# Gate and up projections as seven block products, with two low parts and all weight sums on GpSimd

## What is computed

```python
def conv_ffn(h, prev, w_gate, w_up, conv_w, conv_b, w_down):
    g = h @ w_gate
    gp = jnp.concatenate([prev.astype(g.dtype), g], axis=1)
    c = conv_b
    for j in range(CONV_W):
        c = c + conv_w[j] * gp[:, j:j + t]
    y = (jax.nn.gelu(c) * (h @ w_up)) @ w_down
    return y, gp[:, t:]
```

## Time and profile before

| | |
|---|---|
| median of 3 runs | 2069.16 us (2069.08 to 2069.41) |
| profiled execution | 2069.33 us, of which its span 2067.5 us |
| PE / PE weight load busy | 2038.8 us (99%) / 1797.0 us |
| DVE / ACT / POOL busy | 981.7 us (47%) / 763.9 us (37%) / 198.6 us (10%) |
| mean DMA rate | 106 GB/s |

### The profile page before, as it was taken

The page is one execution under the profiler, slowest core; times in us unless marked ns, Lnnn a source line. Parts: engine busy times, 40 slices in busy tenths (PEclk is TensorE's granted clock), DMA queues, the critical chain, the costliest instruction groups (busy, mean ns, idle before and its releaser), DMA issues.

```text
span 2067.5 us, 30583 instructions
## 1 busy us (share of the span) xinstructions
PE 2038.8 (99%) x12398; PEld 1797.0 (87%) x12398; DVE 981.7 (47%) x1648; ACT 763.9 (37%) x1318; POOL 198.6 (10%) x458
## 2 busy tenths in 40 slices
PE   9999989999999999999999999999999999999997
PEld 7889767987789999999989888799778999999996
DVE  5453664435444443443453467653545444343443
ACT  4222552435344233232244447243534433223232
POOL 3012121000100000000010124210010000000001
PEclk9999999999999999999999999999999999999999
DMA  5324143245622122222221211723572222212221
GB/s 176 124 79 149 52 162 129 92 152 187 243 85 83 62 82 83 91 69 62 76 77 62 82 55 34 275 77 117 197 285 85 65 79 82 78 56 82 82 82 55
DMA packets 111066, 219.42 MB, mean 106 GB/s; under 512 B 7011, under 2 KB 52367, under 8 KB 110862
## 3 DMA queue, kind: packets, MB, share of 16 engines
q1 hardware_dynamic: 91234, 148.00, 21.4%
q0 software_dynamic: 19696, 69.47, 9.9%
HBM read 200.51 MB, written 18.24 MB: 106 GB/s over the span
## 4 chain that ended last, share of the span: by engine, by line
PE 95%; DVE 2%; ACT 2%; issue 1%; DMA 0%; POOL 0%; SPq 0%; DVEq 0%; ACTq 0%; POOLq 0%
PE bank L794 15%; PE bank L796 15%; PE bank L795 15%; PE bank L858 7%; PE bank L860 7%; PE bank L862 7%; PE bank L859 5%; PE bank L861 5%; PE bank L863 5%; PE bank L820 1%; PE bank L1240 1%; PE bank L1256 1%; PE bank L1197 1%; PE bank L1282 1%; PE bank L1293 1%
## 5 line engine op out<-in xcount | busy, mean ns | idle before, releaser
L2093 DVE TENSOR_TENSOR w_lo<-raw,w_hi 128x1024 fp32r<-128x1024 f32 x265 | 319.2, 1220 | 508.9 <-ACT w_hi L1563 505.0
L1563 ACT ACTIVATE w_hi<-raw 128x1024 fp32r<-128x1024 f32 x265 | 275.1, 1054 | 254.6 <-PE bank L796 203.5
L794 PE MATMUL bank<-w_hi,hT_lo 128*128 128x512 f32 x720 | 290.7, 404 | 3.1 <-DVE w_lo L2093 1.9
L858 PE MATMUL bank<-hT_hi,w_lo 128*128 128x384 f32 (+1 forms) x856 | 290.1, 339 | 0.0
L860 PE MATMUL bank<-hT_lo,w_hi 128*128 128x384 f32 (+1 forms) x856 | 289.3, 338 | 0.0
L862 PE MATMUL bank<-hT_hi,w_hi 128*128 128x384 f32 (+1 forms) x856 | 289.3, 338 | 0.0
L796 PE MATMUL bank<-w_hi,hT_hi 128*128 128x512 f32 x720 | 281.9, 391 | 0.0
L795 PE MATMUL bank<-w_lo,hT_hi 128*128 128x512 f32 x720 | 281.2, 391 | 0.0
L859 PE MATMUL bank<-hT_hi,w_lo 128*128 128x256 f32 (+1 forms) x856 | 239.0, 279 | 0.0
L861 PE MATMUL bank<-hT_lo,w_hi 128*128 128x256 f32 (+1 forms) x856 | 239.0, 279 | 0.0
L863 PE MATMUL bank<-hT_hi,w_hi 128*128 128x256 f32 (+1 forms) x856 | 239.0, 279 | 0.0
(11 more groups left out here) (372 smaller groups left out, 2997.4 us busy)
## 6 DMA issues: line engine op xcount, KB each, us to landing
raw<-w_ffn_gate SPq DMA_DIRECT2D x44, 512.0 KB, 4.1
raw<-w_ffn_up SPq DMA_DIRECT2D x44, 512.0 KB, 5.1
raw<-w_ffn_down SPq DMA_DIRECT2D x22, 1024.0 KB, 4.9
kcX<-cache_mem_k POOLq DMA_DIRECT2D x16, 1024.0 KB, 6.1
vcX<-cache_mem_v POOLq DMA_DIRECT2D x16, 1024.0 KB, 6.9
raw<-w_in_even SPq DMA_DIRECT2D x13, 1024.0 KB, 5.6
raw<-w_in_odd SPq DMA_DIRECT2D x12, 1024.0 KB, 5.2
raw<-w_cq SPq DMA_DIRECT2D x8, 1024.0 KB, 7.5
```

What stands on the lines that cost most here:

```text
L794: pe.matmul(out, wl, xh, start=first, stop=False)
L858: pe.matmul(oa, wl, hT_hi[:, k, 0:HA], start=f, stop=False)
L1563: act.activation(w_hi[:, g % W_SLOTS, 0:n], raw[:, q % 2, UNIT * i:UNIT * i + n], ACT.Copy).then_inc(*hi_made.mark(c, u))
L2093: dve.tensor_tensor(w_lo[:, s, 0:n], raw[:, q % 2, UNIT * i:UNIT * i + n], flat(w_hi[:, s, 0:n]), ALU.subtract).then_inc(*lo_made.mark(c, u))
```

## The change

The operands of gate and up are seen as 2 x 2 blocks. The weights of a pair are cut by their input rows (k = 0 to 3, and 4 to 7) and by output tile (f even, f odd); the tokens are cut into the first 320 (`HT`) and the last 320. A scheme of seven products (Strassen's identity in its form with seven products and shared sums) takes the place of the eight. Seven weight units stand for each pair where there were four: A11, A12, A22 are blocks of the loaded weights (`quarter`), and S1 to S4 are sums and differences that POOL forms in fp32 (`weight_sum`), S1 into a buffer of its own and the others in place in `raw`. Each unit is used for gate and for up, with four row blocks each: 7 x 2 x 4 x 3 = 168 matmuls of 320 columns, in 14 banks. ACT still makes all high parts. POOL makes the low parts of S1 and S3 (`weight_low`), DVE those of the other five.

The token side has sums as well, made once in each layer before and during pair 0: t1 and t2 (on DVE) and t3 and n4 (on POOL), each split into high and low. The outputs come back by additions: ACT copies the banks of A11 and A12, POOL adds these two (`first_corner`, "C11"), and DVE makes the rest with `to_sums`, `c22`, `c12` and `c21`, each operation with one operand in PSUM. Now `af` holds up and is multiplied by `cv` in place (`gated`). `FFN_PLAN` sets pairs and groups in the order gu0 gu1 dn0, gu2 gu3 dn1, gu4 gu5 dn2, gu6 gu7 dn3, gu8 gu9 gu10 dn4 dn5. The tiles of pair 0 no longer stand between the last norms; `gate_up` has two transposes between its first banks.

```diff
+FFN_PLAN = [("gu", 0), ("gu", 1), ("dn", 0)]
+for _g in range(1, GROUPS - 2):
+    FFN_PLAN += [("gu", 2 * _g), ("gu", 2 * _g + 1), ("dn", _g)]
+FFN_PLAN += [("gu", FT // 2 - 3), ("gu", FT // 2 - 2), ("gu", FT // 2 - 1), ("dn", GROUPS - 2), ("dn", GROUPS - 1)]
+
+PARTS = ("A11", "A12", "S1", "S2", "S3", "S4", "A22")
+POOL_PARTS = ("S1", "S3")
+HT = TOK // 2
+A_SLOTS = 6
...
-                    sp.wait_ge(*lo_made.at(oc, ou + on - 1))
+                    sp.wait_ge(*lo_made.at(oc, PARTS.index("A22" if ou else "S4") if oc[0] == "gu" else ou + on - 1))
+                    if oc[0] == "gu" and ou == 0:
+                        sp.wait_ge(*lo_pool.at(oc, PARTS.index("S3")))
...
+                def weight_sum(j, part):
+
+                    c = ("gu", l, j)
+                    q0, q1 = LOAD_OF[(c, 0)][0], LOAD_OF[(c, 2)][0]
+                    s1 = sum_at[1 if j else 0][:, :, :]
+                    if part == "S1":
+                        pool.wait_ge(*w_in[q0 % 2].at(q0))
+                        pool.wait_ge(*w_in[q1 % 2].at(q1))
+                        if j == 1:
+                            pool.wait_ge(*xn_made.at(f"ffn{l}", T - 1))
+                        out, a, b, op = s1, quarter(c, 0, 1), quarter(c, 1, 1), ALU.add
+                    elif part == "S3":
+                        out, a, b, op = quarter(c, 0, 1), quarter(c, 0, 0), quarter(c, 0, 1), ALU.subtract
+                    elif part == "S2":
+                        pool.wait_ge(*lo_made.at(c, PARTS.index("A11")))
+                        pool.wait_ge(*pool_done.at("sum", l, j, "S3"))
+                        out, a, b, op = quarter(c, 0, 0), s1, quarter(c, 0, 0), ALU.subtract
+                    else:
+                        pool.wait_ge(*lo_made.at(c, PARTS.index("A12")))
+                        pool.wait_ge(*pool_done.at("sum", l, j, "S2"))
+                        out, a, b, op = quarter(c, 1, 0), quarter(c, 1, 0), quarter(c, 0, 0), ALU.subtract
+                    pool.tensor_tensor(out, a, b, op).then_inc(*pool_done.mark("sum", l, j, part))
+
+                def weight_low(j, part):
+
+                    c, u = ("gu", l, j), PARTS.index(part)
+                    w = FIRST_UNIT[c] + u
+                    lo, hi = (t[:, w % W_SLOTS, :].rearrange("p (q n) -> p q n", n=P) for t in (w_lo, w_hi))
+                    pool.wait_ge(*hi_made.at(c, u))
+                    pool.tensor_tensor(lo, part_source(c, u), hi.bitcast(F32), ALU.subtract).then_inc(*lo_pool.mark(c, u))
...
+                def first_corner(j, key):
+
+                    pool.wait_ge(*lin_a.at(("gu", l, j), (key, "A12")))
+                    dst = gp[0][:, HALO:HALO + HT] if key == "g" else af[0][:, 0:HT]
+                    pool.tensor_tensor(dst, dst, p1[key][:, :], ALU.add).then_inc(*pool_done.mark("C11", l, j, key))
...
+                norm_rstd(f"ffn{l}", [0])
+                norm_rstd(f"ffn{l}", [1])
+                weight_sum(0, "S1")
+                norm_rstd(f"ffn{l}", [2])
+                weight_sum(0, "S3")
+                norm_rstd(f"ffn{l}", [3])
+                weight_sum(0, "S2")
+                norm_rstd(f"ffn{l}", [T - 1])
+                weight_low(0, "S1")
+                weight_sum(0, "S4")
+                pool.wait_ge(*act_done.at("hF", l, T - 1, 1))
+                pool.tensor_tensor(t3F[:, :, :], hF[:, 1, :, HT:TOK], hF[:, 0, :, HT:TOK], ALU.subtract).then_inc(*pool_done.mark("t3F", l))
+                weight_low(0, "S3")
+                pool.wait_ge(*dve_done.at("t2F", l, 1))
+                pool.tensor_tensor(hF[:, 1, :, 0:HT], hF[:, 1, :, 0:HT], t2F[:, :, :], ALU.subtract).then_inc(*pool_done.mark("n4F", l))
+                pool.wait_ge(*act_done.at("prevT", l))
+                for j in range(FT // 2):
+                    more = j + 1 < FT // 2
+                    halo(2 * j)
+                    halo(2 * j + 1)
+                    if j:
+                        weight_low(j, "S3")
+                    first_corner(j, "g")
+                    first_corner(j, "u")
+                    if more:
+                        weight_sum(j + 1, "S1")
+                        weight_sum(j + 1, "S3")
+                    tails(2 * j)
+                    if more:
+                        weight_sum(j + 1, "S2")
+                        weight_low(j + 1, "S1")
+                    tails(2 * j + 1)
+                    if more:
+                        weight_sum(j + 1, "S4")
...
+                def gate_up(j, between={}):
+
+                    c = ("gu", l, j)
+                    for u, part in enumerate(PARTS):
+                        wait_unit(c, u)
+                        if j == 0:
+                            wait_operand(part)
+                        hi, lo = operand[part]
+                        for m, key in enumerate("gu"):
+                            out = lin.open(pe, c, (key, part))
+                            for k in range(KT // 2):
+                                cols = slice(P * (2 * k + m), P * (2 * k + m) + P)
+                                ins = three(out[:, 0:HT], weight(c, u, False)[:, cols], weight(c, u, True)[:, cols], lo[:, k, :], hi[:, k, :],
+                                            k == 0, k == KT // 2 - 1)
+                            ins.then_inc(*lin_full.mark(c, (key, part)))
+                            if (part, key) in between:
+                                between[part, key]()
...
-                for g in range(GROUPS):
-                    for j in group_pairs(g):
-                        c = ("gu", l, j)
-                        for e in range(2):
-                            if j == 0 and e == 0:
-                                continue
-                            cols_tile(c, f"ffn{l}", P * e, ("g", e))
-                            cols_tile(c, f"ffn{l}", 256 + P * e, ("u", e), last=e == 1)
-                    if g:
+                for kind, i in FFN_PLAN[:-1]:
+                    if kind == "gu":
+                        gate_up(i, {("A11", "g"): lambda: norm_tile(nm, T - 2), ("A12", "g"): lambda: norm_tile(nm, T - 1)} if i == 0 else {})
+                    else:
                         for t in range(T):
-                            down(g - 1, t)
+                            down(i, t)
...
+                        if oc[0] == "gu":
+                            act.wait_ge(*lin_full.at(oc, ("u", PARTS[ou])))
...
+                    if f is not None:
+                        gelu(f)
+                    refill_hi(g0 + 4)
+                    if i:
+                        first_product(i, "g")
+                    if f is not None:
+                        gelu(f + 1)
+                    if i:
+                        first_product(i, "u")
+                    if f is not None:
+                        high_a(f)
+                    corner(i, "g")
+                    refill_hi(g0 + 5)
+                    if f is not None:
+                        high_a(f + 1)
+                    corner(i, "u")
+                    if i == 0:
+                        high_t("t3", t3[0][:, :, :], t3F[:, :, :], 0, pool_done.at("t3F", l))
+                    refill_hi(g0 + 6)
+                    if i == 0:
+                        high_t("n4", n4[0][:, :, :], hF[:, 1, :, 0:HT], 0, pool_done.at("n4F", l))
+                    refill_hi(g0 + 7)
+                    refill_hi(g0 + 8)
+                    refill_hi(g0 + 9)
+                    tap0(2 * i)
+                    refill_hi(g0 + 10)
+                    tap0(2 * i + 1)
...
+                def to_sums(j, key):
+
+                    c = ("gu", l, j)
+                    dve.wait_ge(*pool_done.at("C11", l, j, key))
+                    dve.wait_ge(*lin_full.at(c, (key, "S2")))
+                    dve.tensor_tensor(u2[key][:, :], p1[key][:, :], lin.bank(c, (key, "S2"))[:, 0:HT], ALU.add).then_inc(*lin_v.mark(c, (key, "S2")))
+                    dve.wait_ge(*lin_v.at(c, (key, "S2")))
+                    dve.tensor_tensor(p1[key][:, :], u2[key][:, :], lin.bank(c, (key, "S1"))[:, 0:HT], ALU.add).then_inc(*lin_v.mark(c, (key, "S1")))
...
+                sum_t(0)
+                low_ts(0)
+                sum_t(1)
+                low_ts(1)
+                halves(nm, T - 1)
+                for n, (kind, i) in enumerate(FFN_PLAN):
+                    c = (kind, l, i)
+                    g0 = FIRST_UNIT[c]
+                    f = 2 * FFN_PLAN[n - 1][1] if n and FFN_PLAN[n - 1][0] == "gu" else None
+                    if f is not None:
+                        c21(i_before, "u")
+                        taps(f + 1)
+                        gated(f)
+                    if kind == "dn":
+                        if f is not None:
+                            refill_lo(g0 + 4)
+                            low_a(f)
+                            gated(f + 1)
+                            low_a(f + 1)
+                        down(i)
+                        continue
+                    refill_lo(g0 + 4)
```

(24 more changed lines are left out.)

375 lines of the change are left out of this document (277 added, 98 removed).

## The result

The changed kernel takes 2138.42 us (median of 4 runs, 2137.19 to 2139.61), the kernel before 2069.12 on the same chip. The ratio is 1.0337, 95% interval 1.0319 to 1.0355: 69 us slower. The forecast was 2050, the range 2006 to 2084.

The account below looks back on a forecast made before the run. PE, busy 99% of the span, was taken to bound the kernel. From 2069.3 us, 77 came off for less PE work and 59 were added for waits (29.4 a layer), giving 2051, stated as 2050; range 2006 to 2084.

Parts of the forecast that it names:

- start of the FFN (pair 0): Before pair 0: norm scale, transposes and t1 no longer hidden; PE waits 6.5 us a layer, bounds 3 and 9.
- gu3, gu5, gu7, gu9: Second pairs behind a `down`: late sums and low parts make PE wait 2.4 us each, 9.6 a layer.
- gu10: The one third pair behind a `down` in each layer: its chain starts late, PE waits 7.3 us.
- PE's work: Gate and up pairs: 168 matmuls at 0.1467 us, 24.65 us a pair for 28.16; 77 us gained over 22 pairs.
- rival 3: PE takes 320 columns as it takes 384, 29.2 us a pair: 2150 us; chance 0.02.
- what would upset it: A pair's lateness not made good in the `down` behind: all pairs at a 31 us cycle, slower by far.
- rival 2: POOL's 1024 columns slower than 2.05 us; at 2.5, 2091 us; chance 0.22 together with the clock.
- the prediction's rate: Each 0.1 us more per POOL operation of 1024 columns costs 4.6 us a layer, 9.2 in all.
- DVE and POOL exclude each other: DVE operations with two SBUF inputs and POOL's SBUF reads take turns: 27.1 us a pair, over PE's 24.65.
- one chain: From a pair's A22 low part through the next pair's load, sums, low parts to `to_sums`; lateness there makes PE wait.
- rival 1: DVE and POOL hardly contend, so only the FFN start costs: 1998 to 2004 us; chance 0.22 with all between.
- rival 4: Gaps in PE's work lower its granted clock; unpriced, adds to the slow side; shares 0.22 with POOL being slower.

Follow-up runs that it names:

- spread: Against the version with all six weight operations on DVE (2103.49 us): sums placed singly, A12 behind `down` 0 after that group's activations; 2053.20 us, 0.9927 of before.
- the order edit alone: Changed kernel with only A12 of the pair behind `down` 0 moved behind that group's activations, on ACT and DVE; 2127.49 us, 1.0291 of before.
- the halves: Changed kernel with each sum and low part on POOL made as two operations of 512 columns; 2131.95 us, one run.

## Why the prediction was wrong

In its own steps, from PE's timeline in layer 0 (distance from the first matmul of one bank to that of the next, less 1.76 us; over a `down`, less its matmuls). The last three columns are the same for three experiments: POOL as long but reading nothing, POOL idle (both in its weight operations), and all on DVE in the spread order.

```
                          predicted  measured  no reads  idle  spread
start of the FFN (pair 0)     6.5      15.8      11.0    10.8    15.1
gu1                           4         6.2       1.3     0       2.8
down 0                        0        17.2       8.9     6.6     6.5
gu3, gu5, gu7, gu9            9.6      21.7       4.6     0       1.1
gu10                          7.3       7.3       5.9     0       3.4
other downs                   2         3.8      12.0     0       3.8
a layer                      29.4      72        44      17      33
```

Layer 1 has 74 in the measured column. 2069.3 - 77 + 72 + 74 = 2138, the measured time within 1 us. Part of that is luck: the same sum is 4 to 6 us over the measured time in the three experiments, so the account is good to some 6 us. The error is in the waits.

**PE's work was right.** A matmul of 320 columns took 0.1464 us for 0.1467; rival 3 is out.

**`down` 0 was priced at nothing, and this is the largest term that failed.** The prediction gives "some 0.5 late" to the `down` behind each of the other pairs and nothing to this one, and closes with what would upset it, a chain not made good in the `down` behind. It did not ask what the short group covers: 15.4 us of PE against the load of the next pair, which holds DVE's and ACT's queues ahead of the activations, and POOL's sums among them. It cost 17.2 and 17.6 us, 35 of the 88 by which the forecast was off. Without reads on POOL it is 8.9, with the order edit alone 11.0.

**POOL's 1024 columns were mis-sized:** 2.41 us where 2.05 was taken, and that without DVE beside them, the sign that the prediction had named for rival 2. By the prediction's rate (9.2 us for each 0.1) this alone is 33 us, and 2050 becomes 2083. Rival 2 gave 2091 for 2.5. In the trace before, the widest row was half as wide, and the step from 256 to 512 columns (2.0 ns a column) was a poorer guide than the 1.24 us row, which gave 2.5. By the Trainium skill, "GPSIMD Engine Reference", section 3.1, the estimate was 2.3, nearer than 2.05; the trace's 2.41 is a little over it.

**The start was 9.3 us a layer too cheap.** DVE's scale took 3.31 us for 1.29, as the prediction described ("just as DVE wants to scale"), but the two t1 operations behind it also meet POOL (the second meets t3): 2.52 and 3.40 us, where the t2 operations of the same widths take 0.96 and 0.69. With POOL's weight operations gone the start still takes 10.8 us, and PE waited there for `hT_lo` (12.4 us over both layers). About 2.7 of the 10.8 are that second t1, which still meets t3 there, and 2.8 are PE's steps at the lower clock. Without both it would be some 5.3 (an estimate from that trace), so what was too cheap is the contention and the clock, not the chain of steps.

**That DVE and POOL exclude each other was right; one chain did not hold all of it.** The forecast with it (2050) and rival 1 without it (1998 to 2004) differ by some 50 us, and the run without reads gave back 72. In the pairs behind a pair the chain came near: with 2.41 in its own rate gu3, gu5, gu7 and gu9 would have been 18.2 for the 21.7 measured, but gu10 11.6 where 7.3 was measured. So that gu10 came out at the forecast's own 7.3 is luck: two errors cancel. The predicted wait for `p1g` is there in each of these pairs, and is 1.43 us, in gu10 no longer than elsewhere; in gu5, for one, three others stand ahead of it (0.80, 1.12 and 1.34 us, for `af` and `p1u`) that the chain doesn't hold. The rest was paid in places that the chain doesn't pass: the norm's scale and t1, and the activations ahead of the additions that free banks in `down` 0. Single short operations stood for a whole POOL operation there (2.42 us for 128 columns). That whole turns cost more than the sum of both engines' times is not shown: the halves speak against a large part of it.

**The clock (rival 4) had no price, and it was not nothing.** PE's steps at the lower level cost some 16 us over both layers: about 4.6 in pair 0, 2.2 in `down` 0 (the 0.43 us steps at 698.43) and 1.6 in gu10 of layer 0, and as much in layer 1. The prediction said that it had no row for it and that it would add to the slow side. These 16 us are inside the table.

What stays open: why with all on DVE and well spread the kernel is at 2053 and not at the 2018 of POOL idle. By the table it isn't `down` 0, which is the same in both, but the start, gu1, gu10 and the other downs, 3 to 4 us each in a layer. DVE's sums stand in or just ahead of each of these places; no run took them apart.

## What to carry to other kernels

Moving work from DVE to POOL is no relief where POOL then reads SBUF while DVE works with two SBUF inputs: add up both engines' times, and look at each short DVE operation on a path to PE, which here could stand for a whole POOL operation. Before giving work to another engine, put it into the gaps of the first one's own order: here DVE was idle for 53% of the time before and is for 36% in the spread version, the same six operations took half as long on it (1.22 us for 2.41), and the order of the queue was worth 50 us, more than the 35 that leaving POOL gave.

An edit that lengthens or shortens waits can also move PE's granted clock. Before calling a gain small, compare PE's steps in both traces: in the halves some 10 us of it had gone there.

In a queue that runs in order look at what stands behind each instruction that waits for a load, above all where the stage behind it is shorter than elsewhere. A rule of order that is right for one group must be tried on all: the same edit gave 3 to 5 us in `down` 0 of a layer and cost 4 to 6 in each other `down` behind two pairs.

## What the hardware showed beyond expectation

In the rows shown the taking of turns is exact to about 0.1 us and symmetric: at 680.71 DVE stood 1.4 us for POOL, and at 682.10 POOL stood 1.1 for DVE. Halving POOL's operations to 512 columns shortened DVE's first tap from 1654 to 1213 ns, and gave back only 6 of the 72 us. POOL's memset of 1024 columns took 0.95 us and left DVE's first tap at 896 ns, where a subtraction of the same width takes 2.41 and stretches the tap to 1654.
